# Adding the gathered rows of V in four column groups of TensorE, four slots at a time

## What is computed

```python
sc, pos = lax.top_k(cand, PEER_TOPK)          # 8 heads, 16 experts each
idx = jnp.take_along_axis(cidx, pos, axis=-1)
gate = jax.nn.softmax(sc, axis=-1)
ue = jnp.take(u_tab, it, axis=0)              # rows of 1024
ve = jnp.take(v_tab, it, axis=0)
a = jax.nn.gelu(jnp.einsum('td,ted->te', xt, ue))
return jnp.einsum('te,ted->td', gt * a, ve)
```

## Time and profile before

| | |
|---|---|
| three runs | 4637.46, 4648.87, 4656.16 us |
| median | 4648.87 us |
| profiled execution | span 4627.7 us; no other time of this execution is given, and nothing is measured around the span |
| busy share of the span | PE 74%, PEld 33%, DVE 64%, ACT 23%, POOL 62% |
| moved | 1486 MB, mean 321 GB/s, of which the gathers 1342 MB |
| mean granted TensorE clock | 0.935 of full speed |

### The profile page before, as it was taken

The page is one execution under the profiler, slowest core; times in us unless marked ns, Lnnn a source line. Parts: engine busy times, 40 slices in busy tenths (PEclk is TensorE's granted clock), DMA queues, the critical chain, the costliest instruction groups (busy, mean ns, idle before and its releaser), DMA issues.

```text
span 4627.7 us, 39193 instructions
## 1 busy us (share of the span) xinstructions
PE 3424.7 (74%) x9648; PEld 1527.8 (33%) x9648; DVE 2972.4 (64%) x6847; ACT 1072.4 (23%) x2261; POOL 2880.2 (62%) x2564
## 2 busy tenths in 40 slices
PE   8778886678778776677676978946666766667777
PEld 2644653122333332222222546422222222222222
DVE  0279999545566555666664889986666665656662
ACT  1332321121232212121122323211212112121222
POOL 0034555456667676777773545657777777777775
PEclk9889898899999899999998989969999999999999
DMA  7468788989899998999995977879999999999998
GB/s 286 162 224 294 256 298 284 351 314 360 332 354 353 335 370 323 360 376 346 354 377 170 331 257 249 328 258 354 361 355 339 356 360 333 363 341 346 371 370 295
DMA packets 392139, 1486.11 MB, mean 321 GB/s; under 512 B 44108, under 2 KB 45838, under 8 KB 375888
## 3 DMA queue, kind: packets, MB, share of 16 engines
q0 software_dynamic: 368640, 1342.34, 79.5%
q1 hardware_dynamic: 23248, 141.13, 8.0%
HBM read 1480.42 MB, written 2.88 MB: 321 GB/s over the span
## 4 chain that ended last, share of the span: by engine, by line
DMA 32%; PE 25%; DVE 17%; issue 17%; POOL 6%; ACT 3%; POOLq 0%; SPq 0%; DVEq 0%; ACTq 0%
DMA rows_ring<-in_peer_v,idx 19%; DMA rows_ring<-in_peer_u,idx 12%; PE psum L825 12%; POOL rows_ring L548 6%; DVE rows_ring L1366 5%; DVE mix L1380 4%; PE psum L648 4%; PE psum L604 3%; PE psum L770 1%; PE psum L635 1%; DVE small L1288 1%; DMA ring<-in_ada 1%; PE psum L782 1%; PE psum L811 0%; PE psum L597 0%
## 5 line engine op out<-in xcount | busy, mean ns | idle before, releaser
L825 PE MATMUL psum<-rows_ring,diag 128*128 128x512 f32 x4096 | 2067.1, 634 | 901.0 <-DMA rows_ring<-in_peer_v,idx 723.9
L1366 DVE SCALAR_TENSOR_TENSOR rows_ring<-rows_ring,area 128x1024 f32<-128x1024 f32 x1280 | 1562.7, 1225 | 957.9 <-DMA rows_ring<-in_peer_u,idx 935.2
L548 POOL DMA_INDIRECT rows_ring<-in_peer_u,idx x1280 | 1419.7, 1109 | 1084.5 <-DVE rows_ring L1366 431.9
L548 POOL DMA_INDIRECT rows_ring<-in_peer_v,idx x1280 | 1460.3, 1141 | 637.4 <-issue 287.1
L825 PEld LDWEIGHTS psum<-rows_ring,diag 128*128 128x128 f32 x4096 | 730.6, 196 | 2192.0 <-issue 950.6
L1057 ACT ACTIVATE diag<-ident,wts 128x128 f32<-128x128 f32 x1024 | 381.7, 397 | 1515.1 <-PE psum L825 1514.3
L648 PE MATMUL psum<-area,ring 128*128 128x128 f32 (+1 forms) x1344 | 381.8, 443 | 17.1 <-ACT area L919 17.1
L1380 DVE SCALAR_TENSOR_TENSOR mix<-rows_ring,wts,mix 128x1024 f32<-128x1024 f32 x254 | 326.2, 1284 | 8.7 <-DMA rows_ring<-in_peer_v,idx 7.6
L648 PEld LDWEIGHTS psum<-area,ring 128*128 128x128 f32 x1344 | 213.4, 198 | 188.2 <-issue 185.1
L604 PE MATMUL psum<-ring,csil 128*2 128x512 f32 x384 | 176.4, 615 | 21.5 <-DMA ring<-in_ada 21.5
L1049 ACT ACTIVATE acts<-dots 128x16 f32<-128x16 f32 x80 | 17.3, 216 | 555.8 <-DVE rows_ring L1366 555.6
(11 more groups left out here) (174 smaller groups left out, 2473.6 us busy)
## 6 DMA issues: line engine op xcount, KB each, us to landing
ring<-in_ada SPq DMA_DIRECT2D x48, 1024.0 KB, 7.1
ring<-in_win SPq DMA_DIRECT2D x32, 1024.0 KB, 7.7
rows_ring<-in_peer_u,idx POOLq DMA_INDIRECT x1280, 6.1
rows_ring<-in_peer_v,idx POOLq DMA_INDIRECT x1280, 6.2
ring<-in_wout SPq DMA_DIRECT2D x16, 1024.0 KB, 6.7
ring<-in_wq SPq DMA_DIRECT2D x16, 1024.0 KB, 7.3
ring<-in_dft SPq DMA_DIRECT2D x12, 1024.0 KB, 7.7
xT<-in_xT_in SPq DMA_DIRECT2D x1, 2560.0 KB, 15.2
```

The lines of the kernel that those rows point to most:

```text
L548: pool.indirect_dma_start(row(table, k), None, (peer_u, peer_v)[table], bass.IndirectOffsetOnAxis(ap=idx[n][:, k:k + 1], axis=0)).then_inc ...
L825: m = pe.matmul(acc[:, b, :], diag[:, k % 4, :], row(1, k)[:, b * 512:(b + 1) * 512], start=False, stop=False)
L1366: dve.scalar_tensor_tensor(out=row(0, k), in0=row(0, k), scalar=1.0, in1=h_tok[GROUPS[grp][1]][:, bass.ds(t * D_MODEL, D_MODEL)], op0=ALU. ...
```

## The change

Every V row, of context units too, is now added on PE, four slots in one go. A gather for V takes 4 slots of 32 tokens instead of one slot of 128 tokens. Partition 32a+t of gather j of quad g then holds slot 4a+g of token 32j+t. For this, PE first turns each unit's indices and weights (`turn_round`, 16 small matmuls into bank 2), and DVE and ACT copy them out (`places`). ACT spreads the weights over `stacked` (four identity blocks of 32 on top of each other) into four 128x32 matrices. The matmul with gather j writes PSUM partitions 32j to 32j+31, so the four gathers of a quad use four column groups. A quad is 8 matmuls, which wait for all four gathers together, and one `v_free`.

POOL issues four U gathers, then four V gathers. The V gathers of a quad wait for `v_free` of the quad before. The row buffers remain four and four. All loops are unrolled, and `pool_tick` and `dve_tick` are gone. The staging copy (L1038) is gone. The V quads of a unit run later than before: two in step u+1, two in step u+2. The mixers' jobs rotate over five banks, and attention keeps two units in flight with one output bank.

```diff
+PICK_AT = ((0, 1), (2,), (3, 4), (5,))
+QUADS = TOPK // 4
 def step_jobs(grp, u):
-    for p in range(PIECES):
+    for p in range(QUADS):
         jobs += [("dot", grp, u, p)] if u < n else []
-        jobs += [("add", grp, u - 1, p)] if u else []
+        if p == 0 and 0 < u <= n:
+            jobs += [("places", grp, u - 1, 0)]
...
+        m, g = (u - 2, p + 2) if p < 2 else (u - 1, p - 2)
+        if 0 <= m < n:
+            jobs += [("add", grp, m, g)]
...
-BANK = {j: 2 + i % 6 for i, j in enumerate(BANKED)}
+BANK0, BANKS = 3, 5
+BANK = {j: BANK0 + i % BANKS for i, j in enumerate(BANKED)}
...
-                pool.wait_ge(s[("u_free", "v_free")[table]], (u + UNIT0[grp]) * TOPK + k + 1)
-                pool.sem_inc(s["pool_tick"], 1)
+            def fetch_u(v, p):
+                for k in range(4 * p, 4 * p + 4):
+                    if v * TOPK + k >= ROWS:
+                        pool.wait_ge(s["u_free"], v * TOPK + k + 1 - ROWS)
+                    pool.indirect_dma_start(row(0, k), None, peer_u,
...
+            def fetch_v(v, g):
+
+                if v or g:
+                    pool.wait_ge(s["v_free"], v * QUADS + g)
+                for j in range(ROWS):
+                    c = QUADS * j + g
+                    pool.indirect_dma_start(row(1, j), None, peer_v,
...
+            def turn_round(v):
+                pe.wait_ge(s["w_ready"], v + 1)
+                if v:
+                    pe.wait_ge(s["turned_w_ready"], v)
+                for j in range(4):
+                    for a in range(4):
+                        m = pe.matmul(turned[32 * a:32 * a + 32, v % 16, j, :, :], ident[:, 32 * j:32 * j + 32],
+                                      turn[v % IDX_PLACES][:, :, 4 * a:4 * a + 4], start=True, stop=True)
+                m.then_inc(s["turn_mm"], 1)
...
+            def add(v, g):
+                n = v * QUADS + g
+                pe.wait_ge(s["spread_ready"], n + 1)
+                for j in range(ROWS):
+                    pe.wait_ge(row_landed[1][j], 16 * (n + 1))
+                for b in range(2):
+                    for j in range(ROWS):
+                        m = pe.matmul(psum[32 * j:32 * j + 32, b, :], spread[:, n % 2, j, :], row(1, j)[:, b * 512:(b + 1) * 512],
+                                      start=False, stop=False)
+                m.then_inc(s["v_free"], 1)
...
+                for j in range(ROWS):
+                    c = QUADS * j + g
+                    m = act.activation(spread[:, n % 2, j, :], stacked[:], ACT.Copy, scale=turned_w[v % IDX_PLACES][:, c:c + 1])
+                m.then_inc(s["spread_ready"], 1)
```

More of the change, by code:

```diff
@@ L182, in start_jobs @@
 def start_jobs(grp):
[L183 removed]
+    return [("pick", grp, 0, p) for p in range(PICK_PARTS)] + [("gexp", grp, 0, 0)]
 def weave(mixer, experts):
@@ L813, in key, with open_tile @@
                 m.then_inc(s[("ka_mm", "kb_mm")[half]], 1)
[L815 removed]
+            def open_tile(tile):
+                if tile:
+                    pe.wait_ge(s["x_added"], tile)
                 for b in range(2):
                     pe.matmul(acc[:, b, :], zeros[:], cos_sin[:, 0, :], start=True, stop=False)
[L819 to L826 removed]
@@ L838, in close_tile @@
+            def close_tile(grp, tile):
+                for b in range(2):
+                    m = pe.matmul(acc[:, b, :], zeros[:], cos_sin[:, 0, :], start=False, stop=True)
+                m.then_inc(s["acc_mm"], 1)
+                pe.wait_ge(s["acc_read"], tile + 1)
                 for k in range(KC):
@@ L1360, in pick @@
                 assert count[0] == PICK_LINKS[part + 1], count
-            def dot(grp, u, t, p):
-                for k in range(PER_PIECE * p, PER_PIECE * (p + 1)):
-                    dve.wait_ge(row_landed[0][k % ROWS], row_value(u + UNIT0[grp], k))
-                    dve.scalar_tensor_tensor(out=row(0, k), in0=row(0, k), scalar=1.0,
-                                             in1=h_tok[GROUPS[grp][1]][:, bass.ds(t * D_MODEL, D_MODEL)], op0=ALU.mult,
-                                             op1=ALU.mult, accum_out=dots[:, k:k + 1]).then_inc(s["u_free"], 1)
@@ L1384, in weigh, with dot @@
-            def weigh(grp, u):
-                g = u + UNIT0[grp]
-                dve.wait_ge(s["gexp_ready"], g + 1)
+            def dot(grp, u, p):
+                v, t = u + UNIT0[grp], u // PEER_HEADS
+                h = h_tok[GROUPS[grp][1]][:, t * D_MODEL:(t + 1) * D_MODEL]
+                if v and p == 0:
+                    dve.wait_ge(s["gelu_ready"], v)
+                for k in range(4 * p, 4 * p + 4):
+                    dve.wait_ge(row_landed[0][k % ROWS], row_value(v, k))
+                    dve.scalar_tensor_tensor(out=row(0, k), in0=row(0, k), scalar=1.0, in1=h, op0=ALU.mult, op1=ALU.mult,
+                                             accum_out=dots[:, k:k + 1]).then_inc(s["u_free"], 1)
```

315 lines of the change are left out of this document (125 added, 190 removed).

## The result

| | before | changed |
|---|---|---|
| median of 4 runs | 4643.16 us | 5718.53 us |
| lowest to highest | 4636.0 to 4656.16 | 5707.45 to 5724.29 |
| span of the profiled execution | 4627.7 us | 5713.8 us |
| mean granted TensorE clock | 0.935 | 0.68 |

The ratio is 1.231, its 95% interval 1.2284 to 1.2336: 23% slower. The forecast of slower was right, its size was not.

What follows compares the result with a forecast made beforehand. It took closely following gathers at a DMA share near 0.96 to bound the lone stretches, DVE the woven context groups. 202 + 92 + 30 + 40 + 20 − 60 = +324 on 4627.7; median said as 4970 us, range 4700 to 5200.

Steps and rivals of the forecast that it cites:

- The closed ring: V's four buffers: four issues, four landings, addition and release follow one another; 13.5 us a cycle against 11.92.
- First issue to PE's start: First part of V's loop, from POOL's first gather to the fourth landing: 9.0 us, range 8.4 to 9.6.
- The addition: PE's 16 records of a V quad: 3.8 us at the low clock, lower end 1.98.
- The wake-up: From the end of PE's addition to the start of the gather it releases: 0.7 us, range 0.5 to 0.8.
- The rival of two at a time: In PE's quads only two of four column groups overlap: quad 7.2 us, loop 16.9, total 5830; chance 0.12.
- The clock: PE idles some 9 us before each quad, so additions run near half clock, granted 0.5 to 0.6 in lone stretches.
- the rival of full clock: PE stays at full clock in V's loop: loop 11.7 us, total about 4565 us, faster; chance 0.12.
- The landing rival: V's four gathers land faster, in 7.1 us: loop 11.6 even at the low clock, total 4540 us; chance 0.04.
- Latent layer 1: Layer running alone, 128 cycles at 13.5 us instead of 11.92: +202 us.
- starts and closes: Latent groups' starts, more U quads fetched before the first V: +40 us; closing 8 tiles: +20 us.
- Latent layer 0: Its 62 cycles alone: +92 us; its 64 woven cycles at 14.3 us against 13.85: +30, from −20 to +80.
- The context groups: Two woven stretches: DVE's relief could win 80 us each, PE's stops lose 40; taken as −30 each, −60.

Runs made afterwards that it cites:

- before_ring: Kernel before, POOL's order changed to four U then four V gathers, the first V gather waiting until all four V buffers are free: 5707.2 us, ratio 1.231.
- before_order: Kernel before, POOL's order changed to four U then four V gathers, each still waiting for its own buffer only: 5001.5 us, ratio 1.078.
- pairs: Changed kernel, gathers of 2 slots of 64 tokens, two gathers in two column groups, two such sets in turn in the four V buffers: 5066.9 us, ratio 1.092.
- pe_hot: Changed kernel with ten matmuls of zeros into an unused bank after each quad where no mixer is woven in: 5550.6 us, ratio 1.197.
- picks_early: Changed kernel with the last parts of a unit's index search moved ahead of its last dots: 5653.5 us, ratio 1.220.
- single_dots: Changed kernel with the four dots of a job made four separate jobs, so mixer jobs can lie between them: 5587.5 us, ratio 1.204.
- context_off_pe: Changed kernel; in context units DVE waits for and releases V's rows, PE neither waits nor adds, V left out of the sum: 5443.5 us, ratio 1.174.
- context_less_pe: Changed kernel with one of the eight matmuls of each context quad done and seven left out, waits and releases kept: 5656.0 us, ratio 1.219.
- v_double: Changed kernel with eight V row buffers instead of four in latent layer 1, two sets in turn: 5323.3 us, ratio 1.148.

## Why the prediction was wrong

**The closed ring** was the right mechanism: joint release alone brings it into the kernel before (before_ring against before_order), a second set of buffers or two pairs take it away. V's gathers come in fours, each burst released by PE.

**The loop's terms.** First issue to PE's start was taken as 9.0 us, range 8.4 to 9.6, from the earlier trace rows; it measures 10.4 in the mean. Issues did not get closer: 0.94 us and 0.30 between them. Of the 1.1 us above the rows' 9.3, half lies in the issues (first to fourth 4.27 us in the mean, where the earlier trace rows have 3.72) and half in the fourth landing (seen by PE 6.13 us after its issue, where the earlier trace rows have 5.6). The addition was 3.8, is 3.55. The wake-up was 0.7, is 0.46 in the mean and 0.30 in most loops. The loop is 14.4, not 13.5. In the 254 cycles of the prediction's count this is some 230 us.

**The addition's overlap.** Four column groups run fully side by side: 1.92 us at full clock, which four records alone need. The rival of two at a time is refuted. By the ratio of 3.07× for row groups that stood beside it (the Trainium skill, TensorE: Matmul & The Clock Gate, Part 3, "Measured speedup vs the span model") a quad would take an estimated 4.8 us at the low clock; the trace has 3.64. **The clock** fell to 0.50 during additions in the lone loops, as forecast; the rival of full clock is refuted for this kernel, and pe_hot, 20% slower at 0.95, shows that a full clock alone would not have made it faster. **The landing rival** is refuted by 10.4. So is, as a price for this place, the estimated 6.8 us by the Trainium skill's fit (DMA: Bandwidth & Descriptors, "Anatomy of one DMA — SWDGE (gpsimd) path"). The DMA share forecast near 0.85 is 0.79 and 0.81 in the two lone stretches.

**Latent layer 1**: forecast +202 and half of 60 for starts and closes, measured +359. Its plain tiles have 32 loops in 460 us, 14.4 each: 2.4 × 128 is 307 us of it. The first tile has 32 us more, put down to its start, and the last 23.

**Latent layer 0**: forecast +92 alone and +30 woven, measured +187 in the last two tiles and +163 in the first two. Woven tiles are hit by the order (before_order has +72 and +76 there), by the late index (picks_early gives 19 and 33 back) and by the bursts of four dots (single_dots gives 27 back in the second), all costed at nothing there.

**The context groups**: this is the step that failed. The prediction said "If DVE's relief counts, 80 us could be won in each; if PE's stops count, 40 lost. I take −30 each"; measured +187 and +191. It saw that PE is filled and stops in order for quads, and priced that at 40 at most, with no row for the waits. The runs show no gain from DVE's relief: even with the additions off both engines the groups stay 60 us longer than before (context_off_pe). PE's queue costs 127 and 130 in each (the same run), of it 28 and 34 the matmuls (context_less_pe). The rest is waiting for V's rows and for `spread`, with the mixer's jobs behind it in the queue. DVE busy 60 to 70% was forecast there; it was 46%.

**Costed at nothing.** `spread` being ready ahead holds in the lone loops, but not in the woven ones (41 us of waits in the first). Turning costs nothing in the lone loops, and PE waits 18 us for `turn` in the first context group.

So of the miss of 762 us between +324 and +1086, 438 lie in the context groups, 228 in latent layer 0 with its share of starts and closes (350 − 122), and 157 in latent layer 1 (359 − 202), less the 60 forecast for starts and closes. The context groups are the largest step, not the only one: without their 438 the median would have been some 5280 us, still above the range, by the loop's length and by what the woven latent tiles lost.

## What to carry to other kernels

Before buffers are waited for or released together, count the loop: with all buffers in one group no transfer into them overlaps their use, and the pace is the sum of issue, landing, use and release. Splitting the same four buffers into two groups in turn gave the lone pace back, even at TensorE's low clock. Before work is moved to an engine with an in-order queue, price the waits that it brings into that queue and not its busy time alone; here an engine that was 83% busy in that stretch had no room for additions whose inputs come late.

## What was not expected of the hardware

- Four column groups of 32, float32 with 512 columns, took 1.92 us for 16 records, the time of four records into one group (1.98). In pairs, two groups took 1.94 us for 8.
- POOL's issue of a gather takes 0.94 us, but 1.80 and 1.75 where DVE's dot of 128x1024 ran beside it (dots at 4506.46 and 4523.36). In before_ring it was 1.72 at a burst's start. In the whole trace of the change, 1739 gathers met no dot in their first 0.94 us and took 0.94 us in the mean, the longest 1.36; 390 had a dot beside them for at least 0.90 us of it and took 1.52 in the mean. So it goes with the dots, but not with every one. No run takes the dots away, so that they are the cause is not shown.
- From PE's last addition to the gather that it releases it is 0.30 us without the increment (the change, 4520.88 to 4521.18) and 0.81 with it (before_ring, 4325.02 to 4325.83).
- At a mean granted clock of 0.59, near the 1.2 GHz level, a DMA share of 0.96 and 362 GB/s were reached (v_double): the rows' pace did not need TensorE's full clock.
